# Two of three groups of a SwiGLU's down products computed with seven half products instead of eight, on one Trainium2 core

## The reference, cut to what matters

```
x <- LN1(alpha*x + 0.5*SwiGLU_1(x))          # alpha = 2 ** 0.25
z  = x @ w_in ; conv branch, pooling branch, gates -> m
x <- LN2(alpha*x + m @ w_out)
x <- LN3(alpha*x + 0.5*SwiGLU_2(x))
SwiGLU(x) = (silu(x @ wg) * (x @ wu)) @ wd   # wg, wu: 1024 x 2816, wd: 2816 x 1024
```

## Time and profile before

| | |
|---|---|
| time, median of 3 runs | 1081.25 us (1079.03 to 1082.61) |
| profiled execution, its own time | 1081.52 us |
| its span, first to last instruction | 1079.7 us |
| mean granted TensorE clock | 0.994 |
| TensorE matmuls, busy | 1055.2 us, 98% of the span, 8731 |
| VectorE busy | 693.6 us, 64% |
| ScalarE busy | 438.0 us, 41% |
| GpSimd busy | 526.0 us, 49% |

### The profile page before, as it was taken

How to read it: one execution, slowest core, us unless ns; L and a number is a source line. 1 busy time by engine, 2 the same in 40 slices (tenths; PEclk the granted TensorE clock), 3 DMA queues, 4 the chain that set the end, 5 groups by cost and what they waited for, 6 DMA issues and landing times.

```text
span 1079.7 us, 20865 instructions
## 1 busy us (share of the span) xinstructions
PE 1055.2 (98%) x8731; PEld 1048.1 (97%) x8731; DVE 693.6 (64%) x1019; ACT 438.0 (41%) x658; POOL 526.0 (49%) x311
## 2 busy tenths in 40 slices
PE   8999999999999999999999999999999999999996
PEld 7999999999999999999999999988999999999996
DVE  6999921288856865732624336889995026886476
ACT  4555532155553343332322324446555113555234
POOL 4355654255658254754553556225566433556321
PEclk9999999999999999999999999999999999999999
DMA  8133244234345040542322344103434323432402
GB/s 257 35 103 106 75 115 117 79 99 118 96 136 141 1 123 18 144 116 67 114 87 79 112 116 110 40 11 88 118 98 118 88 69 99 117 104 84 121 26 80
DMA packets 195002, 103.30 MB, mean 96 GB/s; under 512 B 4420, under 2 KB 193428, under 8 KB 194901
## 3 DMA queue, kind: packets, MB, share of 16 engines
q1 hardware_dynamic: 194827, 101.85, 33.1%
q10 hardware_dynamic: 82, 0.12, 0.1%
HBM read 99.74 MB, written 2.48 MB: 95 GB/s over the span
## 4 chain that ended last, share of the span: by engine, by line
PE 88%; DVE 7%; ACT 2%; issue 1%; DMA 1%; POOL 0%; ACTq 0%; DVEq 0%; POOLq 0%
PE ps L1342 14%; PE ps L1339 14%; PE ps L1340 14%; PE ps L1322 14%; PE ps L1324 14%; PE ps L1323 14%; DVE x L1198 1%; DVE xl L944 1%; DVE x L1179 1%; PE ps L1385 1%; DMA raw<-in_ffn_wd_dram 1%; DVE form_lo L995 1%; PE ps L1386 1%; PE ps L1445 1%; PE ps L1392 1%
## 5 line engine op out<-in xcount | busy, mean ns | idle before, releaser
L572 POOL TENSOR_TENSOR wl<-raw,wh 128x512 fp32r<-128x512 f32 x120 | 222.6, 1883 | 225.5 <-DVE raw L970 184.5
L618 ACT ACTIVATE wh<-raw 128x1024 fp32r<-128x1024 f32 (+3 forms) x203 | 238.4, 1178 | 185.4 <-DMA raw<-in_ffn_wd_dram 100.0
L1322 PE MATMUL ps<-form_hi,wh 128*128 128x260 f32 x640 | 181.6, 284 | 3.9 <-ACT temps L618 3.9
L1324 PE MATMUL ps<-form_hi,wl 128*128 128x260 f32 x640 | 181.1, 283 | 0.0
L1323 PE MATMUL ps<-form_lo,wh 128*128 128x260 f32 x640 | 180.9, 283 | 0.0
L1339 PE MATMUL ps<-xh,wh 128*128 128x260 f32 x640 | 167.0, 282 | 0.7 <-ACT yp L618 0.7
L1340 PE MATMUL ps<-xl,wh 128*128 128x260 f32 x640 | 166.5, 282 | 0.0
L564 POOL TENSOR_TENSOR wl<-raw,wh 128x1536 fp32r<-128x1536 f32 (+2 forms) x36 | 108.4, 3020 | 103.1 <-ACT wh L618 103.1
L1339 PE MATMUL ps<-hid_hi,wh 128*128 128x260 f32 x544 | 141.9, 282 | 0.0
L1340 PE MATMUL ps<-hid_lo,wh 128*128 128x260 f32 x544 | 141.8, 282 | 0.0
L1322 PE MATMUL ps<-xh,wh 128*128 128x260 f32 x480 | 136.8, 285 | 2.8 <-DVE temps L1002 1.5
(11 more groups left out here) (225 smaller groups left out, 2368.0 us busy)
## 6 DMA issues: line engine op xcount, KB each, us to landing
raw<-in_ffn_wg_dram SPq DMA_DIRECT2D x80, 256.0 KB, 3.3
raw<-in_w_in_dram SPq DMA_DIRECT2D x40, 512.0 KB, 3.9
raw<-in_ffn_wd_dram SPq DMA_DIRECT2D x16, 768.0 KB, 5.8
b<-in_ffn_wu_dram SPq DMA_DIRECT2D x40, 256.0 KB, 3.4
raw<-in_ffn_wu_dram SPq DMA_DIRECT2D x40, 256.0 KB, 3.0
raw<-in_ffn_wd_dram SPq DMA_DIRECT2D x16, 640.0 KB, 5.1
raw<-in_w_out_dram SPq DMA_DIRECT2D x7, 512.0 KB, 4.0
xrow<-in_x_prompt_dram SPq DMA_DIRECT2D x4, 512.0 KB, 5.5
```

What stands on the lines that cost most here:

```text
L572: nc.gpsimd.tensor_tensor(wl_slot[:, s, :], raw_slot[:, s, :], wh_slot[:, s, :].bitcast(F32), ALU.subtract).then_inc(lo_ready, 1)
L618: return nc.scalar.activation(out, in_, ACT.Copy)
L1322: mm(out, hi, vh, start=start and n == 1, stop=False, skip_group_check=more)
L1324: ins = mm(out, lo, vh, start=False, stop=n == count, skip_group_check=more)
```

## The change

The 22 hidden blocks are cut in groups of 8, 6 and 8 (`GROUPS`). TensorE's work in a SwiGLU becomes a list of 28 units (`UNITS`): 20 up units (the pairs of before) and 8 down units. Units 8 to 11 compute the down products of group 0 (output blocks 2j and 2j+1 in one unit, 4 units), units 18 to 21 those of group 1; they take the seven half products too, over 4 blocks a half product for group 0 (84 matmuls a unit) and 3 for group 1 (63 matmuls a unit). The up unit of the next group's first block stands ahead of each four. Group 2 is computed in the plain way (`down_tiles`, `closing`), over 8 blocks instead of 10.

The vectors of a down unit are hidden blocks and sums of them. For every hidden block of groups 0 and 1, VectorE makes such sums (`mid_sums`: one instruction of 128x260 for an even f, three for an odd f), ScalarE rounds them (`round_mid`), and VectorE takes their rests one unit later (`mid_rests`: 3x260 columns for an odd f, 260 for an even one); the last ones of a group are taken at the end of the unit in which the next group's first block is computed. TensorE's Q5 of a down unit waits for them (`mid_ready`).

T1 and T3 of the weights are summed into PSUM banks 6 and 7 (`thirteen_whole`) instead of SBUF, from unit 3 on. T2 and the rest of T1 and T3 read them there. T4 (`last_sum`) is now made behind `rest_thirteen`, and ScalarE rounds T1 and T3 first, right behind its first copy of the unit, and the loaded weights afterwards. GpSimd's three rests of a unit wait for T4 as before.

The results of a down unit are added onto `x32` (`down_first`: the copies `first_p`, 260 columns, and `first_uq`, 520 columns, from SBUF, then two PSUM banks of 260; `down_second` and `down_fourth`: one bank of 260 each, in the next unit). Alpha is no longer a pass of its own: the block starts as 2*alpha*x + product, the factor 0.5 is gone and the norm's epsilon is multiplied by 4 in its place; for the second norm alpha is in the subtraction of the shift. ScalarE's Silu takes the place of Sigmoid and a multiplication by VectorE (`gated`, L1031 and L1035 are gone). GpSimd takes the rests of a down chunk in two instructions of 512 columns instead of one of 1536 or 1280.

The core of the diff (some waits for loads and slots are left out of it; `...` marks jumps):

```diff
-    SPANS = ((2, 12), (12, KF))
-    HELD = (12, KF - 12)
-    DOWN_PAIR = ((3, 0, 2, 1, 3, 0, 2, 1), (3, 0, 1, 3))
+    GROUPS = (8, 6, 8)
+    GROUP_AT = [sum(GROUPS[:g]) for g in range(len(GROUPS))]
+    LAST_GROUP = len(GROUPS) - 1
+    UNITS = [None]
+    for g in range(len(GROUPS)):
+        for f in range(max(GROUP_AT[g], 2), GROUP_AT[g] + GROUPS[g]):
+            UNITS.append(("up", f))
+            if g and f == GROUP_AT[g]:
+                UNITS += [("down", g - 1, j) for j in range(K // 2)]
+    NU = len(UNITS) - 1
...
-                tt(thirteen(raw_slot, n, f), raw_slot[:, b11:b22 + 1:2, :],
-                   b12[:, f % 2, :].unsqueeze(1).broadcast_to([P, 2, HK * P]), ALU.add).then_inc(t13_made, 1)
-                dve.wait_ge(t13_made, pair_no(n, f))
-                tt(raw_slot[:, t2, :], raw_slot[:, t1, :], raw_slot[:, b22, :], ALU.add).then_inc(t2_made, 1)
-                dve.wait_ge(t2_made, pair_no(n, f))
-                tt(raw_slot[:, t4, :], raw_slot[:, t2, :], raw_slot[:, b21, :], ALU.add).then_inc(t4_made, 1)
...
+                whole = thirteen_whole(n, p)
+                tt(whole, slots(raw_slot, slice(b11, b22 + 1, 2), p),
+                   b12[:, p % 2, 0:cols].unsqueeze(1).broadcast_to([P, 2, cols]), ALU.add).then_inc(t13_made, 1)
+                dve.wait_ge(t13_made, no)
+                tt(slots(raw_slot, t2, p), whole[:, 0, :], slots(raw_slot, b22, p), ALU.add).then_inc(t2_made, 1)
+            def last_sum(n, p):
+                no = unit_no(n, p)
+                dve.wait_ge(t2_made, no)
+                tt(slots(raw_slot, t4, p), slots(raw_slot, t2, p), slots(raw_slot, b21, p), ALU.add).then_inc(t4_made, 1)
...
+        def thirteen_whole(n, p):
+            return ps[:, 6:8, 0:kblocks(p) * P] if p > 2 else thirteen(raw_slot, n, p)
...
+                    first = step.on(stt(mid32[:, 1, i, :], fourth_whole(i), -1.0, bank(pair, 1), ALU.mult, ALU.subtract))
+                    tt(mid32[:, 0, i, :], even32[:, 1, :], bank(pair, 1), ALU.subtract)
+                    dve.wait_ge(s.mid_step, first)
+                    tt(mid32[:, 2, i, :], mid32[:, 1, i, :], bank(pair, 0), ALU.add).then_inc(s.mid_made, 1)
+                def mid_rest(f):
+                    i = (f - GROUP_AT[group_of(f)]) // 2
+                    dve.wait_ge(s.mid_round, MID_NO[f])
+                    if f % 2:
+                        ins = tt(mid_lo[:, :, i, :], mid32[:, :, i, :], mid_hi[:, :, i, :].bitcast(F32), ALU.subtract)
+                    if f % 2 == 0 or i == 0:
+                        ins = tt(half(xl[:, i, :], 1), fourth_whole(i), half(xh[:, i, :], 1).bitcast(F32), ALU.subtract)
+                    ins.then_inc(s.mid_ready, 1)
...
+                    a, b = half(x32[:, 2 * j, :], 0), x32[:, 2 * j + 1, :]
+                    onto(p, a, first_p).then_inc(p_taken, 1)
+                    onto(p, b, first_uq).then_inc(u_taken, 1)
+                    dve.wait_ge(p_taken, no)
+                    tt(a, a, bank(q, 0), ALU.add)
+                    dve.wait_ge(u_taken, no)
+                    b = half(b, 0)
+                    tt(b, b, bank(2, q), ALU.add).then_inc(s.part, 1)
...
+                def down_second(p):
+                    dve.wait_ge(w_used, number[n, "P7", p])
+                    y = half(x32[:, 2 * j + 1, :], 1)
+                    tt(y, y, bank((p + 1) % 2, 1), ALU.subtract).then_inc(q_taken, 1)
+                def down_fourth(p):
+                    dve.wait_ge(w_used, number[n, "Q4", p])
+                    onto(p, half(x32[:, 2 * UNITS[p][2], :], 1), bank((p + 1) % 2, 1)).then_inc(s.part, 1)
...
+                    if was[0] == "up":
+                        up_second(p - 1)
+                    elif was[0] == "down":
+                        down_second(p - 1)
+                    f, pair = (was[1], p % 2 if was[0] == "up" else 3) if was[0] != "down" else (None, None)
+                    if p < NU:
+                        weight_sums(n, p + 1)
+                    if f in MID_NO and f % 2 == 0:
+                        mid_rests(f - 1)
+                    if p < NU:
+                        rest_thirteen(n, p + 1)
+                        last_sum(n, p + 1)
+                    if was[0] == "up":
+                        hid_pair(p - 1)
+                    elif was[0] == "down":
+                        down_fourth(p - 1)
+                    if f in MID_NO and f % 2:
+                        mid_sums(f, pair)
+                    elif f is not None and f % 2 == 0 and group_of(f) < LAST_GROUP:
+                        mid_sums(f, pair)
+                    if was[0] == "up" or p == 1:
+                        hid_rest(f, pair)
+                    if now[0] == "up":
+                        gate_first(p)
+                        up_first(p)
+                    else:
+                        down_first(p)
+                    if p < NU:
+                        rest_twenty_four(n, p + 1)
+                    if f is not None and f + 1 in GROUP_AT:
+                        mid_rests(f)
...
+                    act.wait_ge(w_used, number[n, "P1", p])
+                    keep(first_p, x_bank, 1.0, p_taken)
+                    if p < NU:
+                        round_thirteen(n, p + 1)
+                    act.wait_ge(w_used, number[n, "Q5", p])
+                    keep(first_q, z_bank, 1.0, q_taken)
+                    if p < NU:
+                        round_unit(n, p + 1)
+                    if was[0] == "up":
+                        second_gate(p - 1)
+                    act.wait_ge(w_used, number[n, "P6", p])
+                    keep(first_u, x_bank, -1.0, u_taken)
+                    if was[0] == "up":
+                        hid_up(was[1], p % 2)
+                    if p < NU:
+                        round_twenty_four(n, p + 1)
+                    if was[0] != "down":
+                        round_mid(was[1])
+                    if not down:
+                        act.wait_ge(p_taken, no)
+                        nc.scalar.activation(bank((p + 1) % 2, 0), gate_sum, ACT.Silu).then_inc(s.on1, 1)
...
+                    if down:
+                        pe.wait_ge(s.hid_ready, GROUP_AT[UNITS[p][1] + 1] - 1)
+                    half_product("P1", "B11", p, x_bank)
...
+                        pe.wait_ge(u_taken, no - 2)
+                    if down:
+                        pe.wait_ge(s.mid_ready, MIDS[UNITS[p][1]])
+                    half_product("Q5", "T1", p, z_bank)
+                    if p > 1:
+                        fourth(p - 1)
...
+                def fourth(p):
+                    pe.wait_ge(t24_ready, unit_no(n, p))
+                    pe.wait_ge(q_taken, unit_no(n, p))
+                    half_product("Q4", "T4", p, bank((p + 1) % 2, 1), start=False)
...
+                    run_both(DOWN_PAIR[0], [tile(0, k) for k in range(2)], stop=False)
+                    fourth(NU)
+                    run_both(DOWN_PAIR[0], [tile(0, k) for k in range(2, nk - 1)], start=False, stop=False)
+                    pe.wait_ge(lo_ready, lo_no[n, "down", 1])
+                    run_both(DOWN_PAIR[1], [tile(1, k) for k in range(nk - 1)], stop=False)
```

More of the change, by code:

```diff
@@ L348, in size_of @@
                 return 2
[L349 removed]
+            return GROUPS[-1] if what[1] == "down" else K
         free_from = [0] * SLOTS
@@ new lines, in half_product, with second @@
+                def half_product(name, weight, p, out, start=True):
+                    done(run(out, [(block_of((n, weight, p), k), *moving(name, p, k)) for k in range(kblocks(p))],
+                             start=start, more=not start), n, name, p)
+                def fourth(p):
+                    pe.wait_ge(t24_ready, unit_no(n, p))
+                    pe.wait_ge(q_taken, unit_no(n, p))
+                    half_product("Q4", "T4", p, bank((p + 1) % 2, 1), start=False)
+                def second(p):
+                    pe.wait_ge(lo_ready, lo_no[n, "B21", p])
+                    half_product("P2", "B21", p, bank((p + 1) % 2, 0))
@@ L1578, in pair_free @@
+                for p in range(1, NU + 1):
+                    unit(p)
+                down_tiles()
                 def pair_free(i):
```

785 lines of the change are left out of this document (415 added, 370 removed).

## The result

The changed kernel takes 1093.93 us (median of 4 runs, 1092.9 to 1098.56) against 1080.19 us (4 runs, 1079.03 to 1082.61) for the kernel before: a ratio of 1.0125, 95% interval 1.0109 to 1.0141. It is slower by 13.7 us, in spite of 168 matmuls less. The forecast was 1097 us, with a range of its own from 1088 to 1106.

A forecast was written before the change was run, and what follows sets the result against it. TensorE, busy 98% of the span, was taken as the bound, with VectorE just keeping up. 1081.5 - 20.7 + 21 + 5.4 + 5.2 + 0.5 + 5 = 1097.9, 0.3 less against the median: forecast 1097 us, own range 1088 to 1106.

The forecast's parts named there:

- Matmuls saved: Down products in both SwiGLUs: 168 matmuls less at 0.1205 us, with VectorE's dropped instructions 20.7 us saved.
- Down units: Units of groups 0 and 1: VectorE's chain of 11.1 and 9.0 us makes TensorE wait at Q4, 21 us lost.
- the turns: VectorE instructions with two SBUF operands and GpSimd's rests each wait for the other's instruction to end, 1.29 or 0.97 us.
- the excess of a middle unit: TensorE's stall in a down unit between a group's first and last: 1.0 us in group 0, 1.4 in group 1.
- Up units: Up units of groups 0 and 1: VectorE 0.2 us late in 13 units, 1 us at the opening; 5.4 us in all.
- `mid_ready`: Q5 waits for the last sums' rests at a group's end: 1.65 us in group 0, 0.95 in group 1, 5.2 in all.
- Opening: Start of the SwiGLUs: P6's wait shrinks without `gated`, Q3 waits for a later copy; 0.5 us lost in all.
- Closings: Ends of the SwiGLUs: TensorE has 20% less work to cover VectorE's statistics and sums; 5 us lost.
- Loads: Weight loads keep their bytes and no row shows TensorE waiting for one: 0 us.
- Rival 1: Down units: turns with GpSimd hardly bind, VectorE's chain is 8.0 and 7.0 us; 1076 us, chance 0.17.
- The bounds: Smallest and largest total from the bounds of all terms: 1061 to 1128 us.

The follow-up runs named there:

- the slots' run: Out chunks 2 and 3 swap slots in OUT_AT, against the changed kernel: 1088.46 us, ratio 1.0082 to the kernel before.

## Why the prediction was right, point by point

- **Matmuls saved, 20.7 us**: 168 less, and where TensorE is fed a unit of 84 takes 10.09 us, 0.1201 us each. Right.
- **Down units, 21 us**: right in mechanism, 3 to 4 us too large. Without GpSimd's rests 16.8 us are gone; counted unit by unit, 9 to 12 and 19 to 22 take 17.8 us more than their matmuls in both SwiGLUs. The order of the turns is as forecast to 0.2 us: GpSimd's third rest ends at 151.93, and `rest_twenty_four`, in its place from 151.37, ends 1.1 us behind that end, 10.9 us after `down_second` began, where I had 11.1. What was mis-sized is the excess of a middle unit: 1.0 us forecast and 0.7 measured in group 0 (from Q5 to Q4, with the wait, 2.12 instead of 1.44), 1.4 and 1.1 in group 1, where units 19 and 20 take 8.6 and 8.8 us and not 9.0, and 2.7 and 1.8 at group 1's end (unit 22). Unit 21 takes 9.46 us; 0.7 of that is in Q3 and P7 and stays without GpSimd's rests. A row was misread on the way: of the "0.69 to 0.71" beside a running GpSimd, the 0.69 shown in the earlier trace rows (L965) has no PSUM operand and ran before GpSimd began; L1040's 0.71 bears the reading.
- **Up units, 5.4 us**: 4.4 us leave with the rests in all units. The working does not give the term: 0.2 us in 13 units and 1 us are 3.6 in a SwiGLU, and I wrote 2.7. I had put turns into the even f only and 1 us into the opening; the runs show 1.4 us in units 2 and 3 of the first SwiGLU and 0.1 to 0.2 in units 4 to 7, where unit 3 lost its 0.9 to the turns. Group 2, costed at nothing, loses 0.1 us a unit in 5 units of each SwiGLU.
- **`mid_ready`, 5.2 us**: 4.4 us of waits. In unit 8 it is 3.12 us from P1 to Q5 instead of 1.44, in unit 18 2.01 instead of 1.08: 1.68 and 0.93, against 1.65 and 0.95 forecast. But it is no cause of its own: with the wait taken away, the next unit got longer by as much.
- **Opening 0.5 us**: the first P1 comes 0.8 us later, and then to unit 2 it is 11.26 us against 11.24; that P1 came 38.3 to 42.9 us into the span in the profiled executions of the changed kernel and its variants, so 0.8 says little. In the second SwiGLU I had seen neither the gain, 1.5 us, since P1 no longer waits for `gated`, nor the cost: TensorE waits 2.13 us for ScalarE's copy before `form_hi`, the granted clock is 0.68 from 736 to 741 us, where the kernel before keeps 1.00, and unit 1 takes 12.58 us against 11.41.
- **Closings, 5 us**: the step that failed, together with what follows. TensorE waits 0.8 us for the second half's sums (L1320) in the first norm, where it did not wait before, and 5.2 us at the end instead of 4.4: 1.6 us in all. Between the statistics and their spreading I had put 0.7 us of waiting; the stretch went from 3.5 to 2.8 us with the shorter filling and has no wait, so the 3.5 us had been TensorE's own work and not the length of VectorE's chain. For the sums, I had taken the end of VectorE's sums in the kernel before as its earliest possible, less 0.9 us; that it comes earlier still, following TensorE's earlier products, fits but was not tested by a run.
- **Loads, 0**: wrong for one load, 4.4 us in the second norm of this profiled execution (5.5 us by the medians of the slots' run). I wrote that each load is issued when the product before it in its slot has run and took this to be early enough everywhere; I did not follow `OUT_AT`, though it stands in the diff. And in the units a load has so little slack that one moved instruction makes it the bound.

Too much: 3 to 4 us in the down units, 3.4 in the closings, 1 each in the up units and `mid_ready`, 9 in all. Not seen: 4.4 in the second norm, 1 in group 2, 1.2 in the second SwiGLU's first unit, some 7 in all, and against them 1.5 gained at its P1. The low clock in the profile of the kernel before, 1.5 us or so, is in no term. So 1097 lies 3 us above 1094, nearer than its terms deserve: part of that is luck. The bounds were added wrongly too: with every term at its largest the sum is 1116 us, not 1128, and at its smallest 1059, not 1061. Rival 1 (turns do not bind, 1076 us) has its number confirmed by the experiment that takes the turns away, 1077 us, and its condition refuted.

## What to carry to other kernels

A matmul saved is worth its 0.12 us only as long as the other engines' chains, their waits included, stay below TensorE's shorter unit: write these chains down instruction by instruction before counting matmuls. Where VectorE and GpSimd both work from SBUF, cut GpSimd's instructions short and put VectorE's SBUF instructions where GpSimd is idle; each of the two alone brought the time back here to about that of the kernel before. When an instruction is moved into a gap, follow what it then stands behind, and take a slot table in a diff as a schedule of loads: ask of each slot what loads next and when.
